# Moving the low parts of 51 weight chunks from VectorE to GpSimd in a hybrid attention and convolution layer

## Chip, cores and metric

The kernel runs on one core of one Trainium2 chip. The metric is the device time of one launch in microseconds (us). The engines are TensorE (PE in the profile), VectorE (DVE), ScalarE (ACT), GpSimd (POOL) and the queue of SyncE (SP), which issues the loads of the weights.

## The reference, cut to what matters

```python
hn = rms_norm(h_res, norm_mix_gain)            # 528 tokens (16 meta + 512), 1024 channels
part = lambda i: hn @ w_in[:, o[i]:o[i + 1]]   # q, k, v, forget gate, GLU (2048), two merge gates
a = forgetting_attention(q, k, v, part(3) + b_forget) @ w_attn_out     # 16 heads of 64
u = glu_in[..., :1024] * sigmoid(glu_in[..., 1024:])
c = causal_depthwise_conv(u, conv_dw_w, conv_dw_b)                     # 31 taps
c = silu(layer_norm(c)) @ w_conv_out + b_conv_out
h_res = h_res + (sigmoid(part(5)) * a + sigmoid(part(6)) * c) @ w_out
h_res = h_res + square(relu(rms_norm(h_res) @ w_mlp_up)) @ w_mlp_down  # 4096 wide
y = rms_norm(h_res)[:, 16:]                                            # everything float32
```

## The kernel before

**Chunks.** All weights go through TensorE as chunks of 1024 x 128 numbers, held as a tile of 128 x 1024. There are 145, numbered c = 0 to 144. A float32 product is made of three products of type fp32r: each chunk is split into a high part `w_hi` (ScalarE, `high(c)`, L454) and a low part `w_lo` = raw - high (VectorE, `low(c)`, L695), and the input likewise into `in_hi` and `in_lo`. `chunk` (L978) then issues 8 x 3 products of 512 columns (L997), or twice as many of 264 columns where all 528 tokens are wanted (L993). `raw` has four buffers, `w_hi` and `w_lo` have two each. The load of chunk c waits for the high and the low part of chunk c - 4, `high(c)` waits for the raw data and for the products of chunk c - 2, `low(c)` for `high(c)`, and the products for `low(c)` (semaphore `s_lo`).

**Order.** Each engine has its program written out by hand, and semaphores tie them together. Chunk 0 is the forget gate. Chunks 1 to 16 are the GLU stage: for each of eight channel groups m one chunk goes to the sigmoid (ScalarE, into `vT`) and one to the value. VectorE makes `u` from both (L762), and the products of the next group's value chunk wait for that (`s_u`). After that it does `TAPS_EARLY` convolution taps of group m (L749 for the first, L752 for the others), each one `cv = u * tap + cv` over 128 x 512 and each waiting for the one before it.

**Attention.** Chunks 17 to 48 are eight sets of V, Q, K and the attention gate, one set for each pair of heads. Pair step k has eight steps s = 0 to 7, with half a chunk of products in each; between these the attention of pair k - 1 is worked in. In a step TensorE makes scores (L1074 to L1078), VectorE their row maximum (L777), ScalarE the exponential, TensorE transposes it and multiplies it by V, and VectorE scales the result (L791). VectorE fills the rest with `low` and with taps: `TAPS_MID` per group in pair step 0, the rest of group k - 1 in pair step k. Steps k = 8 and 9 use the chunks 49 to 56 of the second merge gate.

**GpSimd.** Before the change it writes the decay rows of the forget gate to DRAM, which waits for VectorE's L771 right after the GLU stage (`s_f` 9), reads rows back for each pair (`rows_back`, after the pair's scores), and adds up the convolution outputs: `add_conv(m)` (L428) waits for the last tap of group m, at the end of pair step m + 1. In the layer norm it also adds squares (L443).

**Afterwards** come the attention output, the convolution output, the merge, and an MLP of 64 chunks.

Of the kernel before, what the change touches and what calls it, by code (L numbers as in the profile page):

```python
# [20 lines left out]
F32 = mybir.dt.float32  # L21
# [7 lines left out]
KT = D // P  # L29
# [21 lines left out]

PAD = TAPS - 1 - META
UW = PAD + T
TAPS_EARLY = 7
TAPS_MID = 1
TAPS_LATE = TAPS - TAPS_EARLY - TAPS_MID
TAPS_STEP = (3, 3, 3, 3, 3, 3, 2, 3)
MID_STEP = (0, 0, 2, 2, 0, 0, 2, 2)
assert sum(TAPS_STEP) == TAPS_LATE and sum(MID_STEP) == KT * TAPS_MID

SQ_POOL = 5
# [25 lines left out]
def build(nc, x, meta_tokens, norm_mix_gain, w_in, b_forget, w_attn_out, b_glu, conv_dw_w, conv_dw_b,  # L87
# [3 lines left out]
    with ExitStack() as ctx:  # L91
# [297 lines left out]
        @block.gpsimd  # L389
        def _(pool):  # L390
            nc.gpsimd.memset(eps_rms[:, :], RMS_EPS).then_inc(s_const, 1)
            nc.gpsimd.memset(ident[:, :], 0.0).then_inc(s_const, 1)
            nc.gpsimd.memset(mask[:, :], 0.0).then_inc(s_const, 1)
            nc.gpsimd.memset(ones[:, :], 1.0).then_inc(s_const, 1)
            nc.gpsimd.memset(mean_w[:, :], 1.0 / D).then_inc(s_const, 1)
            nc.gpsimd.memset(eps_ln[:, :], LN_EPS).then_inc(s_const, 1)
            pool.wait_ge(s_const, 6)
            nc.gpsimd.affine_select(out=ident[:, :], in_=ident[:, :], compare_op=ALU.not_equal, fill=1.0,
                                    base=0, pattern=[[-1, P]], channel_multiplier=1).then_inc(s_const, 1)

            nc.gpsimd.affine_select(out=mask[:, :], in_=mask[:, :], compare_op=ALU.is_ge, fill=MASKED,
                                    base=0, pattern=[[-1, P]], channel_multiplier=1).then_inc(s_const, 1)

            for r0, rows, src in ((0, TAPS, conv_dw_w[0]), (R_BGV, 2, b_glu[0].rearrange("(a d) -> a d", d=D)),
                                  (R_CB, 1, conv_dw_b), (R_LG, 1, conv_ln_gain), (R_LB, 1, conv_ln_bias),
                                  (R_CO, 1, b_conv_out), (R_G2, 1, norm_mlp_gain)):
                pool.dma_start(prow[r0:r0 + rows, :], src).then_inc(s_par, 16)
            pool.dma_start(bf[:, :], b_forget.rearrange("a h -> h a")).then_inc(s_bf, 16)

            pool.wait_ge(s_f, 9)  # L410
            for part in range(2):
                pool.dma_start(decay_dram[part, :].rearrange("(h t) -> h t", t=T),
                               dec_rows[:, part, :]).then_inc(s_decw, 16)
            pool.wait_ge(s_decw, 32)

            def rows_back(pair, slot):
                pool.dma_start(k_b[HD:HD + 2, slot, :, :].rearrange("p h t -> p (h t)"),
                               decay_dram[:, ds(pair * (2 * T), 2 * T)]).then_inc(s_dec[slot], 16)

            rows_back(0, 0)  # L420
            rows_back(1, 1)
            nc.gpsimd.memset(conv_sum[:, :], 0.0).then_inc(s_csum, 1)

            def add_conv(m, it=None):

                wait(pool, s_conv, KT * (TAPS_EARLY + TAPS_MID) + TAPS_LATE * (m + 1), it, 2 * TAPS_LATE)
                wait(pool, s_csum, m + 1, it, 2)
                nc.gpsimd.tensor_tensor(conv_sum[:, :], conv_sum[:, :], feat(cv, count(m, it, 2)), ALU.add).then_inc(s_csum, 1)  # L428

            with pool.Fori(0, PAIRS // 2 - 1) as it:  # L430
                for slot in range(2):
                    pool.wait_ge(s_S, it * 16 + 8 * (slot + 1))
                    rows_back(it * 2 + (slot + 2), slot)
                    add_conv(slot, it)
            add_conv(KT - 2)
            add_conv(KT - 1)

            pool.wait_ge(s_S, 8 * PAIRS)
            nc.gpsimd.memset(sq_sum, 0.0).then_inc(s_sqsum, 1)
            for m in range(SQ_POOL):  # L440
                pool.wait_ge(s_sq, m + 1)
                pool.wait_ge(s_sqsum, m + 1)
                nc.gpsimd.tensor_tensor(sq_sum, sq_sum, prob[:, m % 2, 0:NT], ALU.add).then_inc(s_sqsum, 1)  # L443
# [245 lines left out]
        def _(dve):  # L689
# [65 lines left out]
            with dve.Fori(0, KT // 2) as it:  # L755
                for jj in range(2):
                    m = it * 2 + jj
                    g = N_GLU + 2 * jj
                    low(g + 2, it)
                    dve.wait_ge(s_mm, it * 4 + (g + 2))  # L760
                    dve.wait_ge(s_sig, it * 2 + (jj + 2))
                    V.scalar_tensor_tensor(out=u[:, ds(m * UW + PAD, T)], in0=prod(g + 1, T), scalar=par(R_BGV, m),  # L762
                                           in1=vT[:, :], op0=ALU.add, op1=ALU.mult).then_inc(s_u, 1)
                    dve.wait_ge(s_u, it * 2 + (jj + 2))
                    for j in range(TAPS_EARLY):
                        if j == 3:
                            low(g + 3, it)
                        tap(j, m, it * (2 * TAPS_EARLY) + (jj * TAPS_EARLY + j))

            dve.wait_ge(s_f, 8)  # L770
# [29 lines left out]
            def attention_step(s, k, it=None):  # L800
                if 1 <= k <= PAIRS:
                    row_max(s, k - 1, it)
                if s in (4, 6) and k < PAIRS:

                    c = N_PAIR + 4 * k + s // 2 - 1
                    hi, dst, rows, width, scale, ready, done = (
                        (q_a, q_a, slice(HD, P), NT, HD ** -0.5, s_qh, s_ql) if s == 4 else
                        (k_a, k_b, slice(0, HD), T, 1.0, s_kh, s_kl))
                    for h in range(2):
                        wait(dve, ready, 2 * k + 2, it, 4)  # L810
                        V.scalar_tensor_tensor(out=dst[rows, k % 2, h, :], in0=prod(c, width)[h * HD:(h + 1) * HD, :],
                                               scalar=scale, in1=hi[0:HD, k % 2, h, :].bitcast(F32), op0=ALU.mult,
                                               op1=ALU.subtract).then_inc(done, 1)
                if s % 2 == 0 and k == 0 and s > 0:
                    low(N_PAIR + s // 2 + 1)
                if k == 0:

                    for i in range(sum(MID_STEP[:s]), sum(MID_STEP[:s + 1])):
                        j, m = divmod(i, KT)
                        tap(TAPS_EARLY + j, m, KT * (TAPS_EARLY + j) if j == 0 else KT * TAPS_EARLY + i - KT + 1)  # L820
                elif k <= PAIRS:
                    taps(s, k, it, 0, 1)
                before = (7, k - 2) if s == 0 else (s - 1, k - 1)
                has = k >= 2 if s == 0 else 1 <= k <= PAIRS
                if has:
                    sum_reciprocal(*before, it)
                if 1 <= k <= PAIRS:
                    taps(s, k, it, 1, TAPS_STEP[s])
                if has:
                    head_out(*before, it)  # L830
                if s == 2 and k >= 2:
                    wait(dve, s_ohi, k - 1, it, 2)
                    V.tensor_tensor(feat(mid_lo, count(k - 2, it, 2)), pT6,
                                    feat(mid_hi, count(k - 2, it, 2)).bitcast(F32), ALU.subtract).then_inc(s_olo, 1)

            def pair_step(s, k, it=None):
                c = N_PAIR + 4 * k + s // 2
                attention_step(s, k, it)
                if s % 2 == 0 and k > 0:
                    low(c + 1, it, 8)  # L840

            for k in range(2):
                for s in range(8):
# [5 lines left out]
            for k in (PAIRS, PAIRS + 1):  # L849
                for s in range(8):  # L850
                    if k <= PAIRS:
                        pair_step(s, k)
                        continue
                    if s % 2 == 0:
                        low(N_PAIR + 4 * k + s // 2 + 1)
                    attention_step(s, k)
                    if s == 2:
                        dve.wait_ge(s_mus, 1)
                    for m in {2: range(5), 4: range(5, KT)}.get(s, ()):
                        V.tensor_tensor(feat(cv, m), feat(cv, m), bc[:, 0, :], ALU.subtract).then_inc(s_xc, 1)  # L860
                    for m in {5: (SQ_POOL,), 6: range(SQ_POOL + 1, KT)}.get(s, ()):
                        dve.wait_ge(s_sq, m + 1)
                        dve.wait_ge(s_sqsum, m + 1)
                        V.tensor_tensor(sq_sum, sq_sum, prob[:, m % 2, 0:NT], ALU.add).then_inc(s_sqsum, 1)
# [432 lines left out]
```

## Time and profile before

| | |
|---|---|
| three runs | 983.3, 983.37, 985.15 us; median 983.37 us |
| profiled execution | span 982.9 us, 15041 instructions; its own time beside the span is not recorded, the lowest run is 0.4 us above it |
| TensorE busy | 963.5 us (98%) |
| VectorE busy | 600.2 us (61%) |
| ScalarE busy | 404.1 us (41%) |
| GpSimd busy | 29.9 us (3%) |
| mean granted TensorE clock | 0.997 of full speed |

The span runs from the first to the last instruction. A busy share says how long an engine had an instruction in it and not that it set the end. The waits of an engine say what it stood idle for, and the chain of work is followed back from the last instruction.

### The profile page before, as it was taken

How to read it: one execution, taken by the hardware profiler on the slowest of the kernel's cores; microseconds unless marked ns; L12 is line 12 of the kernel's file. 1: busy time of each engine (PE TensorE's matmuls, PEld its weight loads, DVE VectorE, ACT ScalarE, POOL GpSimd, SP SyncE). 2: the span in 40 equal slices, each digit the busy share in tenths (PEclk: the TensorE clock that was granted, in tenths of full speed). 3: DMA queues.
4: the chain of work that ended last, by engine and by line, in shares of the span. 5: the costliest groups of instructions: out<-in, count | busy, mean ns of one | idle time of the engine just before them, and what ended most of it. 6: DMA issues, size and time to landing. Idle time of an engine off the chain costs nothing.

```text
span 982.9 us, 15041 instructions
## 1 busy us (share of the span) xinstructions
PE 963.5 (98%) x5406; PEld 828.1 (84%) x5406; DVE 600.2 (61%) x856; ACT 404.1 (41%) x703; POOL 29.9 (3%) x45
## 2 busy tenths in 40 slices
PE   5999999999999999999999999999999999999997
PEld 5999998888888888887788888788888888888886
DVE  6566678787787877875876655644344334434433
ACT  6423244454454554543684234532143223323322
POOL 2000010000000000000300000000000000000000
PEclk9999999999999999999999999999999999999999
DMA  7333332121212121212233533323333323332222
GB/s 222 87 95 98 85 90 65 44 65 44 65 43 64 43 64 43 65 44 70 81 105 88 171 96 94 89 86 107 96 95 94 101 85 94 98 107 86 86 86 86
DMA packets 153433, 84.28 MB, mean 86 GB/s; under 512 B 3023, under 2 KB 151503, under 8 KB 153392
## 3 DMA queue, kind: packets, MB, share of 16 engines
q1 hardware_dynamic: 152768, 83.37, 29.3%
q8 instruction: 26, 0.43, 0.2%
q0 software_dynamic: 592, 0.29, 0.2%
q14 instruction: 15, 0.12, 0.0%
q10 hardware_dynamic: 32, 0.07, 0.0%
HBM read 81.55 MB, written 2.16 MB: 85 GB/s over the span
## 4 chain that ended last, share of the span: by engine, by line
PE 95%; DVE 3%; DMA 1%; ACT 1%; issue 0%; SPq 0%; DVEq 0%
PE pj L997 61%; PE pj L993 19%; PE pTO L1103 5%; PE pTO L1101 2%; PE pTO L1089 2%; PE pS L1075 1%; PE pS L1074 1%; DVE cv L860 1%; PE pj L1246 1%; DMA ga<-in_x_dram 1%; PE pj L1021 1%; PE pTO L1087 1%; DVE ga L968 1%; PE pS L1078 0%; PE pTO L1158 0%; PE pTO L1147 0%
## 5 line engine op out<-in xcount | busy, mean ns | idle before, releaser
L454 ACT ACTIVATE w_hi<-raw 128x1024 fp32r<-128x1024 f32 x145 | 152.3, 1051 | 161.1 <-PE pj L997 131.0
L997 PE MATMUL pj<-in_lo,w_hi 128*128 128x512 f32 x512 | 207.3, 405 | 0.0
L997 PE MATMUL pj<-in_hi,w_hi 128*128 128x512 f32 x512 | 205.6, 401 | 0.5 <-DVE w_lo L695 0.5
L695 DVE TENSOR_TENSOR w_lo<-raw,w_hi 128x1024 fp32r<-128x1024 f32 x145 | 178.5, 1231 | 40.8 <-ACT w_hi L454 40.0
L997 PE MATMUL pj<-in_hi,w_lo 128*128 128x512 f32 x512 | 201.5, 394 | 0.0
L752 DVE SCALAR_TENSOR_TENSOR cv<-u,prm,cv (+1 forms) x240 | 180.0, 752 | 21.4 <-DVE cv L752 13.3
L997 PE MATMUL pj<-mid_hi,w_hi 128*128 128x512 f32 x368 | 144.4, 392 | 0.0
L997 PE MATMUL pj<-mid_hi,w_lo 128*128 128x512 f32 x368 | 143.3, 389 | 0.0
L997 PE MATMUL pj<-mid_lo,w_hi 128*128 128x512 f32 x368 | 143.2, 389 | 0.0
L997 PEld LDWEIGHTS pj<-in_hi,w_hi 128*128 128x128 f32 x512 | 96.4, 188 | 22.4 <-DVE w_lo L695 1.0
L997 PEld LDWEIGHTS pj<-in_hi,w_lo 128*128 128x128 f32 x512 | 96.6, 189 | 18.8
L997 PEld LDWEIGHTS pj<-in_lo,w_hi 128*128 128x128 f32 x512 | 96.4, 188 | 17.8 <-issue 0.5
L993 PE MATMUL pj<-in_lo,w_hi 128*128 128x264 f32 x512 | 107.8, 292 | 0.0
L993 PE MATMUL pj<-in_hi,w_hi 128*128 128x264 f32 x512 | 106.5, 289 | 0.0
L993 PE MATMUL pj<-in_hi,w_lo 128*128 128x264 f32 x512 | 104.0, 284 | 0.0
L997 PEld LDWEIGHTS pj<-mid_hi,w_lo 128*128 128x128 f32 x368 | 69.1, 188 | 14.6
L997 PEld LDWEIGHTS pj<-mid_lo,w_hi 128*128 128x128 f32 x368 | 69.1, 188 | 14.4 <-issue 0.2
L997 PEld LDWEIGHTS pj<-mid_hi,w_hi 128*128 128x128 f32 x368 | 69.1, 188 | 14.3 <-issue 0.2
L993 PEld LDWEIGHTS pj<-in_hi,w_hi 128*128 128x128 f32 x512 | 79.4, 188 | 0.2
L993 PEld LDWEIGHTS pj<-in_hi,w_lo 128*128 128x128 f32 x512 | 79.2, 188 | 0.0
L993 PEld LDWEIGHTS pj<-in_lo,w_hi 128*128 128x128 f32 x512 | 78.9, 189 | 0.0
L945 DVE TENSOR_TENSOR res<-pj,res 128x512 f32<-128x512 f32 x30 | 20.7, 692 | 85.4 <-PE pj L997 85.4
(189 smaller groups left out, 1004.2 us busy)
## 6 DMA issues: line engine op xcount, KB each, us to landing
raw<-in_w_in_dram SPq DMA_DIRECT2D x57, 512.0 KB, 3.8
raw<-in_w_mlp_up_dram SPq DMA_DIRECT2D x32, 512.0 KB, 4.0
raw<-in_w_mlp_down_dram SPq DMA_DIRECT2D x32, 512.0 KB, 3.6
raw<-in_w_attn_out_dram SPq DMA_DIRECT2D x8, 512.0 KB, 3.6
raw<-in_w_conv_out_dram SPq DMA_DIRECT2D x8, 512.0 KB, 3.6
raw<-in_w_out_dram SPq DMA_DIRECT2D x8, 512.0 KB, 3.6
ga<-in_x_dram SPq DMA_DIRECT2D x4, 512.0 KB, 7.5
cv<-in_x_dram SPq DMA_DIRECT2D x1, 2048.0 KB, 9.0
```

Source lines behind the costliest of these rows:

```text
L454: A(w_hi[:, c % SPLIT, :], raw[:, c % RAW, :], ACT.Copy).then_inc(s_hi, 1)
L695: V.tensor_tensor(w_lo[:, c % SPLIT, :], raw[:, c % RAW, :], w_hi[:, c % SPLIT, :].bitcast(F32), ALU.subtract).then_inc(s_lo, 1)
L752: V.scalar_tensor_tensor(out=dst, in0=src, scalar=par(j, m), in1=dst, op0=ALU.mult, op1=ALU.add).then_inc(s_conv, 1)
L860: V.tensor_tensor(feat(cv, m), feat(cv, m), bc[:, 0, :], ALU.subtract).then_inc(s_xc, 1)
L945: V.tensor_tensor(feat(res, j), prod(c), feat(res, j), ALU.add).then_inc(s_acc, 1)
L968: V.scalar_tensor_tensor(out=y_tok[:, t, :], in0=y_psum(t), scalar=rstd[:, t:t + 1], in1=gain_bc, op0=ALU.mult, op1=ALU.mult).then_inc(s_y ...
L993: last = mm(prod(c, T)[:, h * HALF:(h + 1) * HALF], wt, src[:, kt * T + h * HALF:kt * T + (h + 1) * HALF], **flags)
L997: last = mm(prod(c), wt, src[:, at:at + NT], **flags)
L1021: last = mm(prod(N_F, T)[:, h * HALF:(h + 1) * HALF], (w_hi, w_hi, w_lo)[what][:, N_F % SPLIT, kt * P:(kt + 1) * P], (in_hi, in_lo, in_hi) ...
L1089: last = nc.tensor.transpose(pT6[:, t * P:(t + 1) * P], prob[:, s % 2, META + t * P:META + (t + 1) * P], ident[:, :])
L1101: mm(dst, pT_meta[:, s % 2, :], v_meta[:, k % 2, h * HD:(h + 1) * HD], start=True, stop=False)
L1103: last = mm(dst, pT[:, s % 2, t * P:(t + 1) * P], v_real[:, k % 2, t * P + h * HD:t * P + (h + 1) * HD], start=False, stop=t == q)
```

## The change

`low` for chunks 3 to 53 is issued by GpSimd; before, VectorE issued it. In GpSimd's own order these lows stand so: sixteen before the decay rows, then chunks 19 and 20 between the landing of the decay rows and the first `rows_back`, then four for each pair step ahead of that step's `rows_back` and `add_conv`, and chunk 53 behind the last `add_conv`. `TAPS_EARLY` goes from 7 to 12, `TAPS_MID` from 1 to 3, and the taps of a pair step from 23 to 16.

```diff
-TAPS_EARLY = 7
-TAPS_MID = 1
+TAPS_EARLY = 12
+TAPS_MID = 3
-TAPS_STEP = (3, 3, 3, 3, 3, 3, 2, 3)
-MID_STEP = (0, 0, 2, 2, 0, 0, 2, 2)
+TAPS_STEP = (2, 2, 2, 2, 2, 2, 2, 2)
+MID_STEP = (3, 3, 3, 3, 3, 3, 3, 3)
 ...
+            def low(c, it=None, per=4):
+                wait(pool, s_hi, c + 1, it, per)
+                nc.gpsimd.tensor_tensor(w_lo[:, c % SPLIT, :], raw[:, c % RAW, :], w_hi[:, c % SPLIT, :].bitcast(F32),
+                                        ALU.subtract).then_inc(s_lo, 1)
+            pool.wait_ge(s_lo, N_GLU + 2)
+            with pool.Fori(0, KT // 2) as it:
+                for j in range(4):
+                    low(N_GLU + 2 + j, it)
             pool.wait_ge(s_f, 9)
 ...
             pool.wait_ge(s_decw, 32)
 ...
+            for j in range(2, 4):
+                low(N_PAIR + j)
             rows_back(0, 0)
             rows_back(1, 1)
 ...
             with pool.Fori(0, PAIRS // 2 - 1) as it:
                 for slot in range(2):
+                    for j in range(4):
+                        low(N_PAIR + 4 * (slot + 1) + j, it, 8)
                     pool.wait_ge(s_S, it * 16 + 8 * (slot + 1))
                     rows_back(it * 2 + (slot + 2), slot)
                     add_conv(slot, it)
-            add_conv(KT - 2)
-            add_conv(KT - 1)
+            for m in (KT - 2, KT - 1):
+                for j in range(4):
+                    low(N_PAIR + 4 * (m + 1) + j)
+                add_conv(m)
+            low(N_AO - 4)
 ...   (VectorE, GLU loop)
-                    low(g + 2, it)
 ...
                     for j in range(TAPS_EARLY):
-                        if j == 3:
-                            low(g + 3, it)
                         tap(j, m, it * (2 * TAPS_EARLY) + (jj * TAPS_EARLY + j))
 ...   (VectorE, pair steps)
-                if s % 2 == 0 and k == 0 and s > 0:
-                    low(N_PAIR + s // 2 + 1)
 ...
-                if s % 2 == 0 and k > 0:
-                    low(c + 1, it, 8)
 ...
                     if s % 2 == 0:
+                        dve.wait_ge(s_lo, N_AO - 3)
                         low(N_PAIR + 4 * k + s // 2 + 1)
```

## Rows read from the trace of the kernel before

**Rows 1.** The page: its span, and its busy time by engine.
```profile
span 982.9 us, 15041 instructions
PE 963.5 (98%) x5406; PEld 828.1 (84%) x5406; DVE 600.2 (61%) x856; ACT 404.1 (41%) x703; POOL 29.9 (3%) x45
```

**Rows 2.** Waits of TensorE: total us, times, longest (first and third of six).
```profile
PE pj L1014 <- DVE v_real L708: 8.4, 1, 8.4
...
PE pS L1182 <- DVE res L864: 1.3, 1, 1.3
```

**Rows 3.** Chain that ended last: start us, us, piece; chunks 18, 19, 20, 22 begin.
```profile
126.36 5.55 PE pj L997 x24
131.91 2.92 PE pj L993 x24
...
138.30 5.56 PE pj L997 x24
...
151.34 0.98 PE pj L997 x4
```

**Rows 4.** Timeline of VectorE, GLU stage: u(0), then u(7) and what follows.
```profile
38.64 0.77 DVE L762 SCALAR_TENSOR_TENSOR u<-pj,prm,vT 128x528 f32 x1 [1.73 <-PE pj L993]
...
120.85 0.77 DVE L762 SCALAR_TENSOR_TENSOR u<-pj,prm,vT 128x528 f32 x1 [2.54 <-PE pj L993]
121.91 0.55 DVE L749 TENSOR_SCALAR cv<-u,prm  x1 [0.29 <-DVE u L762]
122.64 0.75 DVE L752 SCALAR_TENSOR_TENSOR cv<-u,prm,cv  x1 [0.18 <-DVE cv L749]
123.57 0.75 DVE L752 SCALAR_TENSOR_TENSOR cv<-u,prm,cv  x1 [0.18 <-DVE cv L752]
124.24 1.22 DVE L695 TENSOR_TENSOR w_lo<-raw,w_hi 128x1024 fp32r<-128x1024 f32 x1
...
128.83 0.69 DVE L771 TENSOR_TENSOR prob<-o_sb,prob 16x528 fp32r<-16x528 f32 x1
```

**Rows 5.** Timelines of VectorE and GpSimd where both work, layer norm.
```profile
468.84 1.62 POOL L443 TENSOR_TENSOR res<-res,prob 128x512 f32<-128x512 f32 x1 [13.11 <-ACT prob L614]
469.21 1.78 DVE L860 TENSOR_TENSOR cv<-cv,bc 128x512 f32<-128x512 f32 x1
...
478.28 0.68 DVE L860 TENSOR_TENSOR cv<-cv,bc 128x512 f32<-128x512 f32 x1
```

**Rows 6.** Timelines of GpSimd, ScalarE and VectorE between GLU stage and attention.
```profile
132.44 1.01 POOL L417 DMA_DIRECT2D k_b<-decay_dram  x2 [1.67 <-DMA decay_dram<-prob]
...
140.87 1.06 ACT L454 ACTIVATE w_hi<-raw 128x1024 fp32r<-128x1024 f32 x1
145.87 0.31 DVE L777 TENSOR_REDUCE nmax<-pS 128x1 f32<-128x144 f32 x1
...
146.58 1.05 ACT L454 ACTIVATE w_hi<-raw 128x1024 fp32r<-128x1024 f32 x1
```

**Rows 7.** Timelines of VectorE, TensorE, GpSimd, end of pair step 2.
```profile
216.09 1.23 DVE L695 TENSOR_TENSOR w_lo<-raw,w_hi 128x1024 fp32r<-128x1024 f32 x1 [0.56 <-ACT w_hi L454]
216.15 0.22 PE L1078 MATMUL pS<-mask_r,ident_r 128*128 128x128 f32 x1
217.23 0.70 DVE L777 TENSOR_REDUCE nmax<-pS 128x1 f32<-128x528 f32 x1
217.85 0.74 DVE L752 SCALAR_TENSOR_TENSOR cv<-u,prm,cv  x1
219.71 0.49 PE L993 MATMUL pj<-in_hi,w_hi 128*128 128x264 f32 x2
220.63 1.27 POOL L428 TENSOR_TENSOR conv_sum<-conv_sum,cv 128x512 f32<-128x512 f32 x1 [3.09 <-DVE cv L752]
221.24 0.31 DVE L777 TENSOR_REDUCE nmax<-pS 128x1 f32<-128x144 f32 x1 [0.59 <-PE pS L1078]
```

**Rows 8.** Busy time by stretch: us, then each engine's, granted clock, DMA share.
```profile
18.00:21.40 3.40, 3.40 (x18) 3.40 (x17) 1.51 (x2) 0.40 (x1) 0.00 (x0) 0.52 0.65 157
```

More of the change, by code:

```diff
@@ L819, in attention_step @@
                         j, m = divmod(i, KT)
-                        tap(TAPS_EARLY + j, m, KT * (TAPS_EARLY + j) if j == 0 else KT * TAPS_EARLY + i - KT + 1)
+                        tap(TAPS_EARLY + j, m, KT * TAPS_EARLY if j == 0 else KT * TAPS_EARLY + i - KT + 1)
                 elif k <= PAIRS:
```

## Prediction

> **What bounds the kernel now.** I read the page first [rows 1]: TensorE is busy 98% of the span, VectorE 61%, GpSimd 3%. Then the waits of TensorE [rows 2]: six rows, 12.7 us in all, of which 8.4 us is the start, 1.9 us falls before the first product of chunk 0, and only 1.3 us (in the layer norm) is the largest one behind that. The chain that ended last [rows 3] runs through TensorE's products from 26.5 us on almost without another engine. So TensorE is the bound, and VectorE's lows are hidden. Taking work from VectorE has at most some 2 us to win; what counts is whether something new makes TensorE wait. The change offers three places: the GLU stage, where VectorE gets more taps; the passage to attention, where two lows stand behind a trip through DRAM; and the end of each pair step, where a low stands behind `add_conv`.
>
> **How long a low takes on GpSimd.** The trace has none. The nearest row is an add of 128x512 on GpSimd, 1.27 us [rows 7]. Twice the columns give at most 2 x 1.27 = 2.54; below lies VectorE's own 1.22 [rows 4]. The row of the engine itself is nearer, so I take 2.5 us. The Trainium skill (GPSIMD Engine Reference, Elementwise — side-by-side cycle accounting) gives about 2.6 cycles for each element at 1.2 GHz where VectorE needs about one. By that estimate a low would be some 2.2 us plus dispatch; the sum below would be about 6 us smaller.
>
> **What such a low does to VectorE's taps.** [Rows 5] show both engines at work on operands in SBUF. The subtraction at 469.21 took 1.78 us; the same one with GpSimd idle took 0.68 (at 478.28). The GpSimd add from 468.84 ended at 470.46, and the subtraction 0.53 us later, at 470.99. So VectorE did not go slower in part: it stood until GpSimd was through, and GpSimd (1.62 for 1.27) had stood for the VectorE instruction ahead of it. VectorE lost 1.1 us to an add of 1.27. Not everything stands: the row maximum at 221.24, which reads PSUM, took its usual 0.31 us in the middle of a GpSimd add [rows 7]. A tap reads `u` and `cv`, both in SBUF, so I treat it like the subtraction. The Trainium skill has this as a rule (SBUF — State Buffer, Who interferes with whom): a VectorE instruction with two SBUF inputs and a GpSimd instruction that reads SBUF exclude each other for a whole instruction. By that rule, the trace agrees; without it the sum would be rival 1.
>
> A low of 2.5 us followed by a tap of 0.75, overlapping by the 0.28 that the rows leave (1.27 + 0.68 made 1.7), takes 2.97 us. A tap in the GLU loop has a spacing of 0.93 (122.64 to 123.57 [rows 4]). A low under the taps thus costs VectorE 2.97 - 0.93 = 2.04 us, against at best 0.
>
> **A, the GLU stage.** VectorE's round for one group, without lows, by [rows 4]: `u` to the first tap 1.06 (120.85 to 121.91), first to second 0.73, ten more spacings of 0.93, and 0.67 from the start of a tap to the next independent instruction (123.57 to 124.24): 1.06 + 0.73 + 9.30 + 0.67 = 11.76 us. TensorE's round is (120.85 - 38.64) / 7 = 11.74 us. So five more taps in place of two lows fill VectorE to the brim, with nothing left over, and two lows on GpSimd fall under the taps in every round (one after the sigmoid, one after the next value chunk): 11.76 + 2 x 2.04 = 15.84 us. VectorE becomes the bound. u(7) starts at 38.64 + 7 x 15.84 = 149.5 where it was 120.85, 28.7 us later. Chunk 18 waits for it; it began at 126.36 [rows 3] with u(7) done at 121.91, a cover of 4.45 us. A = 28.7 - 4.5 = 24.2 us. What is queued behind: the sigmoid of the next group and the high part after it on ScalarE, both with room.
>
> **B, chunk 19.** Its low stands on GpSimd behind `s_f` 9 and two DMAs to DRAM. L771, which gives `s_f` 9, comes after the last tap of group 7: 149.5 + 11.76 = 161.3. From L771's start to the first instruction behind the landed rows took 132.44 - 128.83 = 3.61 us [rows 4, 6]. So the low starts at 164.9, waits some 0.3 for the tap in progress, takes 2.5, and 0.1 goes to the signal: 167.8. Chunk 19 is due at 131.91 + 24.2 = 156.1. B = 11.7 us. The low was hidden behind chunk 18 before; its cover is gone since it now follows a round trip. `rows_back` moves about 5 us later behind the two lows and has the whole of pair step 0 as cover.
>
> **C, chunk 21.** Shifted by 35.9, its high part ends at 140.87 + 1.06 + 35.9 = 177.8 [rows 6], the low at 180.7 with the same 0.3 and 0.1; chunk 20 ends at 138.30 + 5.56 + 35.9 = 179.8. C = 0.9 us.
>
> **D, chunk 22.** VectorE reaches pair step 0 at 161.9 with 24 middle taps (spacing 0.67 because neighbours belong to different groups: 16.1 us), four low parts of Q and K (about 0.7 each as their tiles are like a tap's, 2.8 us), and three GpSimd lows that cost 2.5 - 0.2 = 2.3 each: 161.9 + 25.8 = 187.7. Only then comes the row maximum of the first scores. The high part of chunk 22 follows it by 0.71 (145.87 to 146.58 [rows 6]) and takes 1.05, the low 2.5 more, with 0.1 for the signal: 192.1. Due is 151.34 + 36.8 = 188.1. D = 4.0 us. It depends on the backlog; without that it is 0.
>
> **E, the end of each pair step.** The low for the next pair's first chunk is issued behind `add_conv`, so behind the last tap. By [rows 7], with VectorE's own low (216.09) gone: the scores end at 216.37, row maximum at 216.45, first tap 0.62 later (217.23 to 217.85) at 217.07, second at 218.00, and there is no third. The add started 0.92 after the start of its last tap (220.63, third tap at 217.85 + 2 x 0.93): 218.92. It ends at 220.20, the low at 222.7, TensorE starts at 222.75 where it started at 219.71. The stall is 3.0 us, and eight pair steps have it (k = 1 to 8, the last before chunk 53): E = 24.0 us. The high part had been ready (the low at 216.09 waited for it), so `add_conv` is what is late. Fewer taps and no lows on VectorE within the step hide under TensorE and give nothing; the other three lows of a step have half a pair step's products as cover.
>
> **F, the clock.** TensorE's granted clock was 0.52, the 1.2 GHz level, from 18.0 to 21.4 [rows 8], right after a stretch of idle time and single transposes, and 1.00 later in spite of a wait of 1.3 us. After B's 11.7 us idle I expect one such fall: half of 3.4 us, 1.6 us. In A it would be free, since TensorE has four us to spare there. At the ends of pair steps I take 0, against 1.6 each.
>
> **The sum.** 24.2 + 11.7 + 0.9 + 4.0 + 24.0 + 1.6 = 66.4 us. The profiled execution's span is 982.9 and the median of the runs 0.5 above it: 982.9 + 66.4 + 0.5 = 1049.8, so 1050 us.
>
> **Rivals.**
> Rival 1: taps do not stand for GpSimd. For it: a tap is another instruction (two operations, a scalar) than those seen held up, and 11.76 meets 11.74. Then A is 0, L771 comes at 132.6, the low of chunk 19 is there at 139.1 against 131.9 (B = 7.2), C = 0.9, D = 0, E = 24, F = 1.6: 33.7 us, 1017 us. Against it: [rows 5].
> Rival 2: dearer lows or a falling clock. With 3.1 us for a low (twice the 1.56 or so of a GpSimd add beside VectorE), 0.6 more each: 14 x 0.6 in A, 0.6 each in B and C, 2.4 in D, 8 x 0.6 in E, 16.8 us: 1067 us. Or the clock falls at each of the eight stalls, 8 x 1.6 = 12.8: 1063 us. The Trainium skill (TensorE: Matmul & The Clock Gate, What's actually happening) says that idling TensorE gets the 1.2 GHz level; [rows 8] agree for one long quiet stretch, and no row here has a stall of 3 us behind the start.
> Rival 3, the other side: VectorE's answers are on TensorE's path after all, hidden in matmuls whose ends are modelled. The row maximum at 217.23 stood 0.78 us behind a low; if each of the 32 even steps paid as much, 25 us come back, more than E. It decides only if A and B also vanish, that is if taps do not stand for GpSimd and the round trip is covered: 983 + 1.6 - 1 = about 983. Against it: TensorE shows no wait for VectorE in the pair steps [rows 2].
>
> **Chances.** The forecast 0.72, rival 1 0.12, rival 2 0.13, rival 3 0.02, anything else 0.01. The forecast alone spans 1038 to 1060 (lows of 2.2 to 2.7 us: 14 + 2 + 3 + 8 of them move the sum by about 8 us each way, and D is the least certain). The range that holds rivals 1 and 2 too is 1014 to 1068. Some 0.2% (2 us) is what a measurement can tell from no change: faster 0.01, same 0.01, slower 0.98.
>
> **What would show it.** In the profile after: taps of more than 0.75 us beside GpSimd lows of about 2.5; TensorE waiting for `u` (L762) in the GLU loop, 4 us in each round once the cover is used; one wait of 11 to 12 us on GpSimd's low at chunk 19; eight waits of 3 us on GpSimd's low at the ends of pair steps, with `add_conv` right ahead. Wrong it would be if taps keep their 0.75 us, if a low on GpSimd is far from 2.5 us, or if TensorE's waits add up to much less than the 66 us.

## The result, and the profile after

The changed kernel takes 1066.61 us (four runs, 1064.55 to 1070.31) against 983.34 us for the kernel before: 1.084 times as long, 95% interval 1.0815 to 1.0864. The forecast was 1050 us with a range of 1014 to 1068: the median lies inside it, near its upper end, and one of the four runs above it. It lies outside the 1038 to 1060 us that the forecast without its rivals spanned. The profiled spans are 1064.9 and 982.9 us, 82.0 us apart; the sum had 66.4.

The page of the kernel after, its span and busy times, and of the slices the TensorE clock. Its line numbers are those of the changed file: `low` on GpSimd is L413, `low` on VectorE L712, the first tap L766, the other taps L769, `u` L778, the decay step L785, the chunk's products L1004 (264 columns) and L1008 (512).

```profile
span 1064.9 us, 15057 instructions
PE 987.8 (93%) x5406; PEld 848.9 (80%) x5406; DVE 594.4 (56%) x805; ACT 403.4 (38%) x703; POOL 159.7 (15%) x96
...
PEclk9999986999899998999999999999999999999999
```

TensorE fell from 98% to 93% of a longer span [rows 1], and its busy time rose by 24 us for the same 5406 products: part of the loss is idle time, part is products at a lower clock. The waits of TensorE in the kernel after (total us, times, longest; five of eleven rows):

```profile
PE pj L1004 <- POOL w_lo L413: 31.4, 8, 14.4
PE pj L1004 <- issue: 17.1, 6, 3.8
...
PE pj L1008 <- POOL w_lo L413: 4.9, 2, 2.5
PE pj L1008 <- DVE u L778: 2.9, 1, 2.9
...
PE pS L1193 <- DVE res L875: 1.3, 1, 1.3
```

Four of them are new beside [rows 2]. The six put down to "issue" stand where the value chunk of a GLU group waits for `u`: each ends 0.1 us after a `u` on VectorE does. In the timeline of TensorE a wait stands in brackets ahead of the product that ended it; these are the last of the GLU stage (chunks 16 and 18), then chunks 19, 21, 25, 29 and 53 (the lines between them are left out):

```profile
136.06 0.78 PE L1004 MATMUL pj<-in_hi,w_hi 128*128 128x264 f32 x2 [3.82 <-issue]
152.23 0.47 PE L1008 MATMUL pj<-in_hi,w_hi 128*128 128x512 f32 x1 [2.92 <-DVE u L778]
174.00 0.81 PE L1004 MATMUL pj<-in_hi,w_hi 128*128 128x264 f32 x2 [14.41 <-POOL w_lo L413]
189.86 0.51 PE L1004 MATMUL pj<-in_hi,w_hi 128*128 128x264 f32 x2 [1.00 <-POOL w_lo L413]
229.57 0.51 PE L1004 MATMUL pj<-in_hi,w_hi 128*128 128x264 f32 x2 [2.62 <-POOL w_lo L413]
273.20 0.81 PE L1004 MATMUL pj<-in_hi,w_hi 128*128 128x264 f32 x2 [2.62 <-POOL w_lo L413]
...
536.24 0.50 PE L1008 MATMUL pj<-in_hi,w_hi 128*128 128x512 f32 x1 [2.38 <-POOL w_lo L413]
```

From these starts and [rows 3] the 82 us fall into the places of the forecast. Chunk 53 began at 454.25 in the kernel before; behind it nothing is lost or won.

| place | lateness after it | lost there | forecast |
|---|---|---|---|
| A, GLU stage, to chunk 18 | 152.23 - 126.36 = 25.9 | 25.9 | 24.2 |
| B, to chunk 19 | 174.00 - 131.91 = 42.1 | 16.2 | 11.7 |
| C, to chunk 21 | 189.86 - 143.86 = 46.0 | 3.9 | 0.9 |
| D, to chunk 22 (starts at 197.62) | 197.62 - 151.34 = 46.3 | 0.3 | 4.0 |
| E, eight ends of pair steps, to chunk 53 | 536.24 - 454.25 = 82.0 | 35.7 | 24.0 |
| F, the clock | contained above: 2.7 in C, 14.8 in E | | 1.6 |

VectorE and GpSimd in the GLU stage of the kernel after, groups 0 and 1, timelines of the two engines:

```profile
38.38 0.77 DVE L778 SCALAR_TENSOR_TENSOR u<-pj,prm,vT 128x528 f32 x1 [3.94 <-PE pj L1004]
39.47 2.38 DVE L766 TENSOR_SCALAR cv<-u,prm  x1 [0.32 <-DVE u L778]
42.04 0.75 DVE L769 SCALAR_TENSOR_TENSOR cv<-u,prm,cv  x1 [0.19 <-DVE cv L766]
...
46.71 2.62 DVE L769 SCALAR_TENSOR_TENSOR cv<-u,prm,cv  x1 [0.18 <-DVE cv L769]
...
39.18 2.39 POOL L413 TENSOR_TENSOR w_lo<-raw,w_hi 128x1024 fp32r<-128x1024 f32 x1 [1.30 <-ACT w_hi L471]
46.11 2.68 POOL L413 TENSOR_TENSOR w_lo<-raw,w_hi 128x1024 fp32r<-128x1024 f32 x1 [4.54 <-ACT w_hi L471]
```

A tap of 0.75 us takes 2.62 beside a low, and the next one starts 2.80 us after it (forecast 2.97). The first tap, which reads only one tensor from SBUF, took 2.38 where it had taken 0.55 [rows 4]; that was not forecast.

The passage to attention in the kernel after, VectorE and GpSimd:

```profile
163.09 0.69 DVE L785 TENSOR_TENSOR prob<-o_sb,prob 16x528 fp32r<-16x528 f32 x1
163.71 8.02 DVE L769 SCALAR_TENSOR_TENSOR cv<-u,prm,cv 128x512 f32<-128x512 f32 x12
171.77 1.41 DVE L825 SCALAR_TENSOR_TENSOR q_a<-pj,q_a 64x512 fp32r<-64x512 f32 x2
...
164.08 1.01 POOL L422 DMA_DIRECT2D decay_dram<-prob  x2 [17.06 <-DVE prob L785]
166.50 7.44 POOL L413 TENSOR_TENSOR w_lo<-raw,w_hi 128x1024 fp32r<-128x1024 f32 x1 [1.42 <-DMA decay_dram<-prob]
```

Here a low of 2.4 us took 7.44. VectorE ran twelve middle taps in a row, undisturbed (8.02 us, 0.67 each), and the low ended 2.2 us after the last of them. VectorE did not wait for GpSimd, GpSimd waited for VectorE.

The end of pair step 1 in the kernel after, GpSimd: the low of chunk 25 starts as the add ends.

```profile
225.87 1.27 POOL L440 TENSOR_TENSOR conv_sum<-conv_sum,cv 128x512 f32<-128x512 f32 x1 [1.23 <-DVE cv L769]
227.10 2.33 POOL L413 TENSOR_TENSOR w_lo<-raw,w_hi 128x1024 fp32r<-128x1024 f32 x1
```

The clock behind waits, busy time by stretch of the kernel after (columns as in [rows 8]); the first stretch begins with chunk 19, then come four of the eight ends of pair steps:

```profile
174.00:179.50 5.50, 5.50 (x25) 5.50 (x26) 5.50 (x6) 0.00 (x0) 4.25 (x4) 0.50 0.59 160
273.20:278.60 5.40, 5.40 (x25) 5.40 (x26) 1.89 (x4) 0.21 (x2) 0.00 (x0) 0.50 0.38 100
362.50:368.00 5.50, 5.50 (x32) 5.39 (x32) 1.88 (x4) 1.76 (x5) 0.00 (x0) 0.69 0.33 95
450.90:456.00 5.10, 5.07 (x23) 5.07 (x24) 1.88 (x4) 0.00 (x0) 0.00 (x0) 0.50 0.37 103
495.40:501.00 5.60, 5.60 (x32) 4.64 (x33) 2.00 (x5) 2.04 (x5) 0.68 (x1) 1.00 0.35 94
```

The clock fell in six of the eight places. In four it had fallen before the wait was over, and the products behind ran at the 1.2 GHz level for 5.2 to 5.7 us. In the other two (229.57 and 362.47) it fell one to two microseconds behind the wait, for 3.4 us: hence the mean of 0.69. In the last two places it stayed full.

### The profile page after: what moved, and what is told of

Read it like the earlier page. It is cut to its first block, busy times and chain, and to the rows that moved or that the text cites. A ratio compares the mean times of both kernels' runs of the same rounds, so it can differ in the third digit from the quotient of the medians.

```text
span 1064.9 us, 15057 instructions
## 1 busy us (share of the span) xinstructions
PE 987.8 (93%) x5406; PEld 848.9 (80%) x5406; DVE 594.4 (56%) x805; ACT 403.4 (38%) x703; POOL 159.7 (15%) x96
## 4 chain that ended last, share of the span: by engine, by line
PE 77%; DVE 13%; issue 4%; POOL 3%; DVEq 1%; DMA 1%; ACT 1%; SPq 0%; POOLq 0%
PE pj L1008 54%; PE pj L1004 10%; DVE cv L769 9%; PE pTO L1114 4%; POOL w_lo L413 2%; PE pTO L1112 2%; PE pTO L1100 2%; PE pS L1086 1%; PE pS L1085 1%; DVEq L769 1%; PE pj L1257 1%; DVE cv L871 1%; DMA ga<-in_x_dram 1%; PE pTO L1098 1%; DVE cv L766 1%
## 5 line engine op out<-in xcount | busy, mean ns | idle before, releaser
L769 DVE SCALAR_TENSOR_TENSOR cv<-u,prm,cv (+1 forms) x240 | 228.3, 958 | 22.9 <-DVE cv L769 15.2
L471 ACT ACTIVATE w_hi<-raw 128x1024 fp32r<-128x1024 f32 x145 | 152.5, 1052 | 167.9 <-PE pj L1008 130.9
L1008 PE MATMUL pj<-in_hi,w_hi 128*128 128x512 f32 x512 | 206.2, 403 | 8.3 <-POOL w_lo L413 4.9
L1008 PE MATMUL pj<-in_lo,w_hi 128*128 128x512 f32 x512 | 207.9, 406 | 0.0
L1008 PE MATMUL pj<-in_hi,w_lo 128*128 128x512 f32 x512 | 202.2, 395 | 0.0
L413 POOL TENSOR_TENSOR w_lo<-raw,w_hi 128x1024 fp32r<-128x1024 f32 x51 | 129.8, 2546 | 286.4 <-ACT w_hi L471 285.0
L1004 PE MATMUL pj<-in_hi,w_hi 128*128 128x264 f32 x512 | 114.1, 306 | 48.5 <-POOL w_lo L413 31.4
L1008 PE MATMUL pj<-mid_hi,w_hi 128*128 128x512 f32 x368 | 144.4, 392 | 0.0
L1008 PE MATMUL pj<-mid_hi,w_lo 128*128 128x512 f32 x368 | 143.3, 389 | 0.0
L1008 PE MATMUL pj<-mid_lo,w_hi 128*128 128x512 f32 x368 | 143.2, 389 | 0.0
L712 DVE TENSOR_TENSOR w_lo<-raw,w_hi 128x1024 fp32r<-128x1024 f32 x94 | 116.1, 1235 | 33.5 <-ACT w_hi L471 31.5
L1004 PEld LDWEIGHTS pj<-in_hi,w_hi 128*128 128x128 f32 x512 | 85.6, 204 | 51.6 <-issue 26.9
L1008 PEld LDWEIGHTS pj<-in_hi,w_hi 128*128 128x128 f32 x512 | 96.8, 189 | 30.7 <-POOL w_lo L413 5.1
L1004 PE MATMUL pj<-in_lo,w_hi 128*128 128x264 f32 x512 | 114.5, 307 | 0.0
L1008 PEld LDWEIGHTS pj<-in_hi,w_lo 128*128 128x128 f32 x512 | 97.0, 189 | 18.9
L1008 PEld LDWEIGHTS pj<-in_lo,w_hi 128*128 128x128 f32 x512 | 96.7, 189 | 18.0 <-issue 0.5
L1004 PE MATMUL pj<-in_hi,w_lo 128*128 128x264 f32 x512 | 109.8, 298 | 0.0
L1004 PEld LDWEIGHTS pj<-in_hi,w_lo 128*128 128x128 f32 x512 | 85.5, 203 | 0.0
L1004 PEld LDWEIGHTS pj<-in_lo,w_hi 128*128 128x128 f32 x512 | 85.2, 203 | 0.0
L548 ACT ACTIVATE pT_meta<-pTO 16x128 f32<-16x128 f32 x64 | 17.2, 268 | 171.0 <-PE pTO L1100 171.0
L1008 PEld LDWEIGHTS pj<-mid_hi,w_lo 128*128 128x128 f32 x368 | 69.1, 188 | 14.5
L1008 PEld LDWEIGHTS pj<-mid_hi,w_hi 128*128 128x128 f32 x368 | 69.1, 188 | 14.4 <-issue 0.2
```

The costliest lines, as they stand in the source:

```text
L413: nc.gpsimd.tensor_tensor(w_lo[:, c % SPLIT, :], raw[:, c % RAW, :], w_hi[:, c % SPLIT, :].bitcast(F32), ALU.subtract).then_inc(s_lo, 1)
L471: A(w_hi[:, c % SPLIT, :], raw[:, c % RAW, :], ACT.Copy).then_inc(s_hi, 1)
L548: A(pT_meta[:, s % 2, :], pO7[0:META, 0:P], ACT.Copy).then_inc(s_pm, 1)
L712: V.tensor_tensor(w_lo[:, c % SPLIT, :], raw[:, c % RAW, :], w_hi[:, c % SPLIT, :].bitcast(F32), ALU.subtract).then_inc(s_lo, 1)
L769: V.scalar_tensor_tensor(out=dst, in0=src, scalar=par(j, m), in1=dst, op0=ALU.mult, op1=ALU.add).then_inc(s_conv, 1)
L1004: last = mm(prod(c, T)[:, h * HALF:(h + 1) * HALF], wt, src[:, kt * T + h * HALF:kt * T + (h + 1) * HALF], **flags)
```

## The experiments

Each kernel is compared with the kernel before on the same chip, where that took 984.7 to 984.8 us. Ratios are to that, with their 95% intervals. The changed kernel itself was timed on another chip, where the kernel before took 983.34 us; differences between it and the kernels below are uncertain by such 1 to 2 us.

**One place undone at a time, and all three.** `e1_glu7`: 7 early taps again, lows still on GpSimd.

```diff
-TAPS_EARLY = 12
+TAPS_EARLY = 7
-TAPS_STEP = (2, 2, 2, 2, 2, 2, 2, 2)
+TAPS_STEP = (3, 3, 3, 3, 3, 2, 2, 2)
```

> The changed kernel, but with 7 early taps per channel group and 23 - 2 = 21 late ones; all 51 lows stay on GpSimd and the 3 middle taps stay. Theory: VectorE's round in the GLU loop is 15.8 us because 12 taps alone fill TensorE's 11.74 and two lows hold VectorE up by 2 us each; with 5 taps less it is 11.1 us, so no wait for u, A = 0 (was 25.9). The tail of the GLU loop ends earlier, chunk 19 is then late by some 12 us at most. About 24 to 30 us faster than the changed kernel: 1036 to 1043 us. Rival (TensorE waits there for GpSimd's low, not for the taps): the GLU waits stay and the time stays within 5 us of 1066.

1036.2 us, 1.052 (1.0496 to 1.0543). As expected: no wait for `u` is left, the wait before chunk 19 fell to 8.84 us because VectorE got to the decay step earlier (its low still took 7.44 us), the rest stayed.

`e2_order19`: GpSimd makes the lows of chunks 19 and 20 ahead of its wait for the decay step.

```diff
+            for j in range(2, 4):
+                low(N_PAIR + j)
             pool.wait_ge(s_f, 9)
...
-            for j in range(2, 4):
-                low(N_PAIR + j)
             rows_back(0, 0)
```

> The changed kernel, but GpSimd makes the lows of chunks 19 and 20 before it waits for the decay rows. Theory: the 14.4 us wait before chunk 19 is made of the round trip to DRAM behind VectorE's last tap (about 9 us of it) and of a low that takes 7.4 us instead of 2.4. Both go: chunk 19 starts without a wait, 14 to 18 us faster than the changed kernel, 1049 to 1053 us; some of it may return as a wait for the row maximum of pair step 1 (up to 4 us). Rival (chunk 19 waits for VectorE's 24 middle taps in any case): at most 5 us faster.

1060.75 us, 1.0781 (1.0762 to 1.08): 6 us won where I expected 14 to 18. The rival was nearly right. A wait of TensorE in this kernel, before chunk 20:

```profile
176.49 0.76 PE L1008 MATMUL pj<-in_hi,w_hi 128*128 128x512 f32 x1 [11.14 <-DVE q_a L825]
```

Chunk 20 needs VectorE's low part of Q, which stands behind twelve middle taps, and those behind the whole backlog of the GLU stage. With chunk 19's wait gone this one appears. B had two causes side by side, each enough for most of it.

`e3_low_first`: on GpSimd the low of the next pair's first chunk goes ahead of `rows_back` and `add_conv`.

```diff
+            low(N_PAIR + 4)
             with pool.Fori(0, PAIRS // 2 - 1) as it:
                 for slot in range(2):
-                    for j in range(4):
+                    for j in range(1, 5):
                         low(N_PAIR + 4 * (slot + 1) + j, it, 8)
...
-                for j in range(4):
+                for j in range(1, 5):
                     low(N_PAIR + 4 * (m + 1) + j)
                 add_conv(m)
-            low(N_AO - 4)
```

> The changed kernel, but the low of the next pair's first chunk stands ahead of rows_back and add_conv on GpSimd. Theory: all eight waits of 2.4 to 2.75 us at the ends of pair steps go, and the stretches at the 1.2 GHz level behind them too: 35.7 us of the pair steps come back, 1029 to 1033 us. If only the waits go and the clock falls for another reason: 20 us, about 1046 us. Rival (the low is late because its high part is): no change, 1066 us.

1030.84 us, 1.0474 (1.0456 to 1.0491): 35.8 us won, and the table has 35.7 for E. All eight waits are gone, and so is the low clock; busy time of the pair steps in this kernel:

```profile
190.00:500.00 310.00, 310.00 (x2043) 271.13 (x2043) 196.97 (x356) 151.43 (x368) 89.62 (x47) 1.00 0.20 56
```

`e4_all_three`: the three edits together.

> All three edits in one: 7 early taps, lows 19 and 20 before the decay rows, the next pair's low ahead of add_conv; 51 lows still on GpSimd. Theory: the three places account for all of the 82 us, so it takes the time of the kernel before within 3 us: 981 to 987 us. Rival (GpSimd lows cost something everywhere, by holding up VectorE's row maxima and taps in the pair steps): 990 us or more.

992.7 us, 1.0088 (1.0071 to 1.0104). This is what the rival said (990 us or more), though for another reason: 8 us over the kernel before are left. TensorE waited 4.43 us for the low of chunk 20, which took 7.4 us, again beside a row of twelve middle taps (VectorE's row began at 132.50):

```profile
135.33 7.40 POOL L413 TENSOR_TENSOR w_lo<-raw,w_hi 128x1024 fp32r<-128x1024 f32 x1 [4.84 <-ACT w_hi L471]
```

**The middle taps.** `e5_all_lows_before_taps` is e4 with `TAPS_EARLY`, `TAPS_MID`, `TAPS_STEP` and `MID_STEP` of the kernel before.

> The 51 lows on GpSimd in the order of e4_all_three, but all taps as in the kernel before (7 early, 1 middle, 23 late). The 7.9 us that e4 is above the kernel before I put down to the 24 middle taps: 12 of them in a row kept GpSimd's low out for 5 us (7.4 us for 2.4) and put off the first row maximum. With 8 middle taps both go: 983 to 987 us. Rival (lows on GpSimd cost in the pair steps or in the GLU loop): 989 us or more.

987.69 us, 1.004 (1.0027 to 1.0053), just above the expected 983 to 987. The 51 lows on GpSimd in a good order cost 3 to 4 us. One new wait is left, 2.07 us before chunk 21, whose low follows the decay rows. It does not beat the kernel before, and no version here does.

`e6_mid1_order19` is e2 with one middle tap per group.

```diff
-TAPS_MID = 3
+TAPS_MID = 1
-TAPS_STEP = (2, 2, 2, 2, 2, 2, 2, 2)
-MID_STEP = (3, 3, 3, 3, 3, 3, 3, 3)
+TAPS_STEP = (3, 2, 2, 2, 3, 2, 2, 2)
+MID_STEP = (0, 0, 2, 2, 0, 0, 2, 2)
```

> As e2_order19 (lows 19 and 20 before the decay rows), but with 1 middle tap per group in place of 3 (8 taps in pair step 0, 18 late), 12 early taps stay. Theory: in e2 chunk 20 waited 11.1 us for VectorE's low part of Q, which stood behind 12 middle taps of 0.67 us; with 4 ahead of it that wait is near 5.7 us, and a stretch at 1.2 GHz stays: 1053 to 1057 us against 1060.75. Rival (the wait is for L785 and the GLU taps ahead of it alone): 1060 us.

1056.54 us, 1.0729 (1.0714 to 1.0745), and the wait for the low part of Q is 5.83 us: as expected.

**What GpSimd does to VectorE, by itself.** `e7_probe_two_inputs` is the kernel before with sixteen GpSimd subtractions that nobody's result needs; in `e8_probe_memset` they are memsets.

```diff
...
+            for j in range(2 * KT):
+                pool.wait_ge(s_hi, N_GLU + 2 + j + 1)
+                pool.wait_ge(s_probe, j + 1)
+                nc.gpsimd.tensor_tensor(ga[:, 2 * D:3 * D], ga[:, 2 * D:3 * D], ga[:, 3 * D:4 * D],
+                                        ALU.subtract).then_inc(s_probe, 1)
```

> The kernel before, with sixteen extra GpSimd subtractions of 128x1024 on a tile nobody needs, one beside each chunk 3 to 18; nobody waits for them but the decay rows. Theory (a GpSimd instruction that reads two operands and VectorE's taps or lows exclude each other): taps and lows of VectorE take up to 2 us more beside them, VectorE's round in the GLU loop goes from 9.2 us of work to some 13.3, over TensorE's 11.74, and the kernel gets 5 to 12 us slower. Rival (the loss in the changed kernel comes from who waits for whom): no change, within 1 us of the kernel before.

> As e7, but the sixteen extra GpSimd instructions are memsets of 128x2048, which only write (about 2 us each by the 0.55 us of 128x512). Theory (it is the shared way to read that is held): taps keep their 0.75 us and the time stays within 1 us of the kernel before. Rival (any GpSimd work holds VectorE up): slower by 3 to 10 us, as e7.

e7: 995.17 us, 1.011 (1.0096 to 1.0125), 10.5 us slower without any change in who waits for whom; this is inside the expected 5 to 12. e8: 990.31 us, 1.0056 (1.0042 to 1.0071), 5.6 us slower, which I had not expected. VectorE in e7 (here L702 is `low`, L756 the first tap, L759 the others, L769 `u`):

```profile
61.88 3.41 DVE L702 TENSOR_TENSOR w_lo<-raw,w_hi 128x1024 fp32r<-128x1024 f32 x1
65.22 0.75 DVE L769 SCALAR_TENSOR_TENSOR u<-pj,prm,vT 128x528 f32 x1
66.26 2.26 DVE L756 TENSOR_SCALAR cv<-u,prm  x1 [0.29 <-DVE u L769]
...
74.23 2.63 DVE L759 SCALAR_TENSOR_TENSOR cv<-u,prm,cv  x1 [0.18 <-DVE cv L759]
```

VectorE and GpSimd in e8, the same place, then two taps beside a memset:

```profile
60.59 1.22 DVE L702 TENSOR_TENSOR w_lo<-raw,w_hi 128x1024 fp32r<-128x1024 f32 x1
64.83 1.81 DVE L756 TENSOR_SCALAR cv<-u,prm  x1 [0.29 <-DVE u L769]
...
71.41 0.75 DVE L759 SCALAR_TENSOR_TENSOR cv<-u,prm,cv  x1 [0.18 <-DVE cv L759]
72.34 0.75 DVE L759 SCALAR_TENSOR_TENSOR cv<-u,prm,cv  x1 [0.18 <-DVE cv L759]
...
60.06 1.81 POOL L416 MEMSET ga<- 128x2048 f32 x1 [6.13 <-ACT w_hi L461]
64.55 1.81 POOL L416 MEMSET ga<- 128x2048 f32 x1 [2.67 <-ACT w_hi L461]
71.20 1.81 POOL L416 MEMSET ga<- 128x2048 f32 x1 [4.84 <-ACT w_hi L461]
```

Beside a memset the low keeps its 1.22 us and the taps with two inputs their 0.75. The first tap stands for the memset too (1.81 for 0.55). The low two taps behind it comes later by that, and TensorE waits 0.42 us for it once in every GLU round. So an instruction with two tensors in SBUF stands only for a GpSimd instruction that reads, while the first tap, of another kind, stands for either.

**The taps without the lows.** `e9_taps12_lows_vector`: the changed kernel, with the lows of chunks 3 to 18 on VectorE, as they were.

```diff
...
+                    low(g + 2, it)
                     dve.wait_ge(s_mm, it * 4 + (g + 2))
...
                     for j in range(TAPS_EARLY):
+                        if j == 3:
+                            low(g + 3, it)
```

> The changed kernel, but VectorE makes the lows of chunks 3 to 18, where it made them before; 12 early and 3 middle taps, GpSimd makes chunks 19 to 53. Theory: VectorE's round is 11.76 us for the taps and 2 x 0.87 for lows slipped in between taps = 13.5 us, against 15.8 with the lows on GpSimd. So it still is over TensorE's 11.74, A is 7 x 1.76 - 4.5 = 7.8 us in place of 25.9, the passage to chunk 19 stays as it is (some 16 us): 1047 to 1052 us. It shows that the taps alone would have cost 8 us and that a low is dearer for VectorE on GpSimd than on VectorE. Rival (moving the lows off VectorE did relieve it): slower than the changed kernel, over 1066 us.

1052.82 us, 1.0664 (1.0623 to 1.0704), just above the expected 1047 to 1052 (one of the four runs took 1045.69). VectorE's round is 13.8 us (`u` at 81.31 and 95.08) where I had 13.5. The places came out otherwise than I expected, and partly made up for each other: chunk 18 began at 142.57, 16.2 us late and not 7.8, because TensorE waits for VectorE's low in every round (mostly 1.8 us) before it would wait for `u`; and chunk 19 at 159.96, so the passage lost 11.9 us and not 16. With twelve taps a low is cheaper for VectorE when VectorE makes it (1.22 us, a good part of it between taps) than when GpSimd does (2 us of standing still): 14 us over the kernel.

**Why GpSimd did not get its turn.** `e10_middle_taps_one_op` makes the middle taps plain additions of two tensors; it leaves out the multiplication by the tap's weight, so it does not compute the layer. `e11_middle_taps_chained` keeps the taps and orders them so that each waits for the one before.

```diff
-                        j, m = divmod(i, KT)
-                        tap(TAPS_EARLY + j, m, KT * TAPS_EARLY if j == 0 else KT * TAPS_EARLY + i - KT + 1)
+                        m, j = divmod(i, TAPS_MID)
+                        tap(TAPS_EARLY + j, m, KT * TAPS_EARLY + i)
```

> The changed kernel, but the 24 middle taps of pair step 0 are plain additions of two tensors (no multiplication by the tap weight: this part of the convolution is changed). They stay 24 instructions in a row that don't depend on their neighbours. Question: why the low of chunk 19 took 7.4 us beside them, when GpSimd's adds got their turn after each subtraction in the layer norm. If it is the kind of instruction (tap with a scalar against plain tensor operation), the low takes 2.5 to 3.5 us here and chunk 19 starts 4 to 5 us earlier: 1060 to 1063 us. If it is the unbroken row, the low takes 6.5 to 7.5 us and the time stays within 2 us of 1065.

> The changed kernel, but the 24 middle taps go group by group, three of one group after another, and each waits for the one before it, as the early taps do. Question as in e10: the low of chunk 19 waited out a row of 12 taps that start before the last one has ended, while lows beside chained taps got their turn after one tap. If a gap between VectorE's instructions is what lets GpSimd in, the low of chunk 19 takes 2.5 to 3.2 us here in place of 7.4, chunk 19 starts about 4.5 us earlier, and one or two us of it are lost again to the slower chain ahead of the parts of Q and K: 1060 to 1063 us. If not, the low takes over 6 us and the time is 1065 to 1069 us.

e10: 1065.39 us, 1.0812 (1.0794 to 1.083), the low took 6.72 us. e11: 1066.68 us, 1.0831 (1.0805 to 1.0856), the low took 2.51:

```profile
166.49 2.51 POOL L413 TENSOR_TENSOR w_lo<-raw,w_hi 128x1024 fp32r<-128x1024 f32 x1 [1.42 <-DMA decay_dram<-prob]
```

So the kind of instruction does not decide; waits between the taps let GpSimd in. Chunk 19 began at 169.05, five microseconds earlier than in the changed kernel. VectorE, now the one held up, came later with the parts of Q and K (new waits of 0.3 and 2.4 us), and chunk 22 began at 195.59, two microseconds earlier. In the time that does not show: the runs spread from 1063.85 to 1068.85, and in the profiled one the clock fell behind seven of the eight waits of E, not six. The 1060 to 1063 us of my expectation missed.

## Why the prediction was right, and where it was off

**The low on GpSimd** was sized at 2.5 us; the 51 took 2.55 us on average and 2.39 in the middle. By the Trainium skill's page (GPSIMD Engine Reference, Elementwise — side-by-side cycle accounting) it would have been 2.2 us and some dispatch; the measured median lies between that and the 2.5 us.

**Taps stand for GpSimd** (A): right. VectorE's round after the first is (151.32 - 56.20) / 6 = 15.85 us against the 15.84 that the sum gave. That they agree to 0.01 us is in part luck: the spacing of a tap beside a low ran from 2.67 to 3.02 us (2.97 in the sum), and the gap ahead of the next `u` up to 0.86 (0.67). The loss was 25.9 for 24.2, as the first round took 17.8: three lows fell under it, one of them on the first tap, which I had counted as free. The sum's cover of 4.45 us is misread by a little: u(7) ended at 120.85 + 0.77 = 121.62 [rows 4], and 121.91 is the start of the tap behind it; 30.5 us of lateness of u(7) against 25.9 of chunk 18 make the cover 4.6. e7 shows the mechanism with nothing else changed, e1 that 7 taps leave room for it. Rival 1 is refuted. That the low clock is free here was right too: it was 0.95 on average from 56 to 152 us, and VectorE set the pace. The Trainium skill (SBUF — State Buffer, Who interferes with whom) names both cases, two SBUF inputs against a GpSimd read, and instructions like `tensor_scalar` in a two-port mode against any GpSimd use; the traces of e7 and e8 agree (1.22 us and 0.75 us beside a memset, 1.81 for the first tap).

**The round trip ahead of chunk 19** (B): right in place, 16.2 for 11.7. VectorE came to the decay step at 163.09 (forecast 161.3), the low began 3.4 us later (3.6). The step that failed is "waits some 0.3 for the tap in progress": it waited 5 us for a row of taps. e11 shows it: with waits between the taps the same low took 2.51 us.

**C and D together** were 4.2 for 4.9, but not for the reasons given. C's wait for GpSimd was 1.00 us as forecast (0.9); the other 2.9 of C are nearly all chunk 19 at the 1.2 GHz level (9.06 us from its start to chunk 20's, against 6.39), which F had priced at 1.6. D was 0.3 in place of 4.0: VectorE had no backlog left, it even stood idle for 4.84 us before the parts of K at 184.77. One reason is that its first twelve middle taps held GpSimd up and not the other way round; the other is that chunks 19 to 21 came later than forecast.

**The ends of the pair steps** (E): the waits were 2.4 to 2.75 us, 20.9 in all, for eight times 3.0. Right, and e3 shows the cause, GpSimd's order. The term that was mis-sized is F at these places, "I take 0": the clock fell behind six of the eight waits and cost 35.7 - 20.9 = 14.8 us. Counted directly, half of 22 us (the products of four places at the 1.2 GHz level) and half of 2 x 3.4 us give 14.4. That is most of what the sum lacked. The prediction had it as half of rival 2, at 8 x 1.6 = 12.8 us. Rival 2's other half, dearer lows, did not happen, so that its 1067 us is the measured time is luck. In e3, without the waits, the clock stays at 1.00 through all pair steps. The Trainium skill (TensorE: Matmul & The Clock Gate, What's actually happening) gives an idling TensorE the 1.2 GHz level; the trace agrees in direction, and the price comes from this trace.

The account closes to within the 1 to 2 us of the comparison: the three edits alone bring 30, 6 and 36 us, all three 74, the middle taps 5 more (e4 to e5), and 3 to 4 us stay.

## What to carry to other kernels

An engine that is mostly idle is not free to take work: ask what else stands in its own order ahead of the result (here an add behind the last tap, and a trip through DRAM), and whether it takes away the memory access of the engine that it should relieve. A VectorE round that already fills TensorE's has no room for even one GpSimd operation that makes VectorE stand. A short new wait of TensorE can cost more than its length, since products behind it can run at the lower clock level (35.7 us for 20.9 us of waits here): count it at every place.

## What the runs showed that was not expected

GpSimd can be kept out by VectorE for long. Beside a row of twelve VectorE instructions, each starting before the last ended, a low that came 2.8 us into the row took 7.44 us in the changed kernel and in e1, 7.40 in e4, and 7.17 in e9 (3.1 us into the row). In e2 one that came 4.5 us into the row took 5.74. In each case it ended 2.2 us after the row. Beside chained taps a low took 2.4 to 2.9. But in the layer norm of the kernel before [rows 5], and beside rows of six taps, a GpSimd instruction that came in the first 0.7 to 1.4 us of the row got its turn after one VectorE instruction, and in e5 a low that came 2.4 us into a row of four got in at the fourth tap (the low took 2.35 us, the tap 3.32). What decides between these cases stays open; only the kind of instruction (e10) and the effect of a gap (e11) were tried.

The granted clock does not fall behind every short wait. In the changed kernel it fell behind six waits of 2.6 to 2.75 us and not behind two of 2.50 and 2.38 us, where the products behind have 512 columns. Neither the length nor the products explain that: in e1, e2, e9, e10 and e11 it fell at both of these last places too (waits of 2.5 and 2.4 us, the same products), and it stayed full behind a wait of 2.6 us once each in e1 (331.62), e2 (355.02) and e11 (227.76). Over the kernels with all eight waits it fell at six to eight of them. What decides was not found, so F is a price that differs from one kernel to the next, and the 14.8 us hold for this trace.
